# Thirteen kinds of head groups placed with no dense slice in front of them, in a one-core hybrid recurrent decoder step

## The reference, cut to what matters

```python
# layer 0: gated DeltaNet (8 heads) || GLA (4 heads); layer 1: Mamba-2 SSD (16 heads) || RG-LRU (1024 channels)
for li in range(DEPTH):
    xn = _rmsnorm(h, w['norm_g'][li])
    u = xn @ w_in                      # one wide input projection of the layer
    y = heads(u, states)               # conv, decay matrices, chunk products, state updates
    h = h + y @ w_out                  # output projection
    gate = jax.nn.sigmoid(_rmsnorm(h, w['ple_norm'][li]) @ w['ple_w_gate'][li])
    h = h + gate * (p[li] @ w['ple_w_proj'][li])
```

## Time and profile before

| | |
|---|---|
| median of 3 runs | 2558.11 us (2557.02 to 2559.59) |
| the profiled execution | 2557.48 us |
| its span | 2555.7 us |
| TensorE busy / VectorE / ScalarE / GpSimd | 2445.7 / 1253.8 / 952.5 / 382.6 us |
| mean granted TensorE clock | 0.986 of full speed |
| DeltaNet heads | about 103 to 744 us of the span |
| GLA heads | about 744 to 1094 us |
| SSD pairs | about 1617 to 1885 us |

### The profile page before, as it was taken

One profiled execution on the slowest core, in us unless ns is written; L12 is line 12 of the kernel. 1 busy time (PEld: TensorE's weight loads), 2 busy tenths in 40 slices (PEclk: granted clock), 3 DMA queues, 4 the chain that ended last, 5 costly groups with the idle time before them and its releaser, 6 DMA issues.

```text
span 2555.7 us, 52677 instructions
## 1 busy us (share of the span) xinstructions
PE 2445.7 (96%) x22783; PEld 2308.7 (90%) x22783; DVE 1253.8 (49%) x2299; ACT 952.5 (37%) x1531; POOL 382.6 (15%) x590
## 2 busy tenths in 40 slices
PE   7999999999999999999999999999999979999996
PEld 6998888888889999889999999988899979999996
DVE  6644554545544654622343455556655562243332
ACT  5423443234433443432342253333344552243222
POOL 3101111010100101111111111222212111111111
PEclk8999999999999999999999999999999989999998
DMA  9333333333343543643233333333344445223221
GB/s 237 98 96 99 107 93 104 91 94 95 106 118 97 154 141 101 195 164 92 87 90 111 106 109 93 110 110 113 107 122 119 143 152 170 84 82 100 79 85 72
DMA packets 382712, 289.13 MB, mean 113 GB/s; under 512 B 25444, under 2 KB 347758, under 8 KB 381969
## 3 DMA queue, kind: packets, MB, share of 16 engines
q1 hardware_dynamic: 341424, 172.53, 24.9%
q0 software_dynamic: 24640, 81.69, 10.1%
q10 hardware_dynamic: 16416, 31.55, 3.4%
HBM read 229.15 MB, written 57.28 MB: 112 GB/s over the span
## 4 chain that ended last, share of the span: by engine, by line
PE 83%; DVE 5%; ACT 4%; DMA 4%; issue 2%; POOL 0%; SPq 0%; ACTq 0%; DVEq 0%; POOLq 0%
PE psd L562 67%; PE psw L585 2%; PE psw L584 2%; PE psw L605 1%; PE psw L655 1%; PE psw L590 1%; DMA raws<-uT_scratch 1%; PE psw L633 1%; DMA w_raw<-in_ab_w_in_dram 1%; DMA uT_scratch<-mix 1%; PE psw L641 1%; DVE arena L1926 1%; DMA mix<-in_x_prompt_dram 1%; PE psw L627 1%; DMA yT_scratch<-extra 1%
## 5 line engine op out<-in xcount | busy, mean ns | idle before, releaser
L562 PE MATMUL psd<-xh,w_hi 128*128 128x272 f32 x5056 | 1110.7, 301 | 27.7 <-DVE xl L1718 15.4
L562 PE MATMUL psd<-xh,w_lo 128*128 128x272 f32 x5056 | 1051.6, 290 | 0.0
L562 PE MATMUL psd<-xl,w_hi 128*128 128x272 f32 x5056 | 1049.8, 289 | 0.1
L562 PEld LDWEIGHTS psd<-xh,w_hi 128*128 128x128 f32 x5056 | 800.3, 190 | 83.9 <-issue 42.9
L562 PEld LDWEIGHTS psd<-xl,w_hi 128*128 128x128 f32 x5056 | 800.6, 190 | 0.0
L562 PEld LDWEIGHTS psd<-xh,w_lo 128*128 128x128 f32 x5056 | 796.7, 190 | 0.2 <-issue 0.2
L1664 DVE TENSOR_TENSOR w_lo<-w_raw,w_hi 128x512 fp32r<-128x512 f32 x632 | 437.7, 708 | 416.0 <-ACT w_hi L1121 415.0
L1121 ACT CAST w_hi<-w_raw 128x512 fp32r<-128x512 f32 x632 | 377.9, 615 | 671.6 <-PE psd L562 565.2
L2519 POOL TENSOR_TENSOR states<-states,extra 128x544 f32<-128x544 f32 x59 | 80.0, 1356 | 524.8 <-ACT extra L1176 524.8
L2453 POOL DMA_DIRECT2D raws<-uT_scratch x59 | 36.5, 619 | 635.9 <-DMA uT_scratch<-mix 541.6
L2332 DVE TENSOR_TENSOR extra<-psd,rstd 128x544 f32<-128x544 f32 x32 | 23.2, 724 | 156.2 <-PE psd L562 139.2
(11 more groups left out here) (510 smaller groups left out, 2320.7 us busy)
## 6 DMA issues: line engine op xcount, KB each, us to landing
w_raw<-in_ab_w_in_dram SPq DMA_DIRECT2D x224, 256.0 KB, 3.0
w_raw<-in_cd_w_in_dram SPq DMA_DIRECT2D x148, 256.0 KB, 3.2
w_raw<-in_ple_w_gate_dram SPq DMA_DIRECT2D x128, 256.0 KB, 3.1
uT_scratch<-mix ACTq DMA_DIRECT2D x85, 272.0 KB, 2.5
w_raw<-in_ab_w_out_dram SPq DMA_DIRECT2D x64, 256.0 KB, 2.9
w_raw<-in_cd_w_out_dram SPq DMA_DIRECT2D x64, 256.0 KB, 3.0
raws<-uT_scratch POOLq DMA_DIRECT2D x40, 272.0 KB, 3.2
hT_scratch<-arena POOLq DMA_DIRECT2D x8, 1088.0 KB, 10.7
```

The lines of the kernel that those rows point to most:

```text
L562: mm = pe.matmul(out[:, D0 + HALF * half:D0 + HALF * (half + 1)], w[:, r, k % QH, :], x[:, k, HALF * half:HALF * (half + 1)], start=(k == ...
```

## The change

Thirteen kinds of groups get the weight 0 in the sharing of slices. Their target is then that of the group in front of them, so they follow it with no dense slice between. There are 71 such groups: 5 in each of 8 DeltaNet heads, 3 in each of 4 GLA heads, 2 in each of 8 SSD pairs, and 3 in `bc`. Starts and ends of the units stay where they are, and so does the number of slices and of all instructions. The slices taken from in front of these groups go to the other groups of the same unit in proportion to their weights. The order of the groups is unchanged.

```diff
+TOGETHER = {("dn", "ssk"), ("dn", "bbc"), ("dn", "qk"), ("dn", "vt"), ("dn", "ys"), ("gla", "v0"), ("gla", "o1"), ("gla", "sb1"),
+            ("ssd", "dmB"), ("ssd", "ys"), ("bc", "bts"), ("bc", "cb1"), ("bc", "cb3")}
...
                 mine = [n for (v, n, _, _) in GROUPS if v == u]
-                weight = [FILL.get((u, n), FILL.get((u[0], n), 1.0)) for n in mine]
+                weight = [0.0 if (u[0], n) in TOGETHER else FILL.get((u, n), FILL.get((u[0], n), 1.0)) for n in mine]
```

## The result

The changed kernel takes 2560.36 us (median of 20 runs), the kernel before 2556.14 us (median of 20 runs beside them): ratio 1.0021, 95% interval 1.0011 to 1.0030, so 5.4 us slower, from 2.8 to 7.7 (the medians themselves lie 4.2 us apart). The profiled execution took 2561.76 us with a span of 2559.9 (before: 2557.48 and 2555.7). The forecast was +6.8 us. But the sum behind it is not the sum in the trace: single terms are off by up to 5 us and cancel. That the total landed so close is luck.

The account below looks back on a forecast made before the run. TensorE, busy 96% of the span, was taken as the bound, so its order of work counts. Terms -1.8 + 4.5 + 2.1 - 0.5 + 2.5 = +6.8 us gave 2564.9 against the median; range 2557.5 to 2572.

Parts of the forecast that it names:

- joints: Term for all 71 joints between groups: only tiling changes, 0.1 us each, are saved; -1.8 us, bounds 0 and -14.2.
- selector: SSD pairs 2, 4, 6: ebc loses two slices of cover, so three waits for selp grow 1.5 us each; +4.5 us.
- DeltaNet's waits: DeltaNet heads: new t1 waits and odd-head losses against the x5 and x6 waits going; +2.1 us, from -2.8 to +6.
- waits of GLA and of the output projection's first slices: GLA heads: waits at l0 and o0 go, sb0 and the projection's first slices wait longer; -0.5 us, -2.2 to +2.
- clock: Half-rate clock after longer selector waits: one new low stretch (+1.3), one longer (+1.2); +2.5 us, from 0 to +7.
- Four `sb0` with `sb1` stay in one narrow tiling and save both changes, 0.2 each: GLA heads: each of four pairs saves two tiling changes of 0.1 us; 0.8 us in all.
- Eight `ss` with `ys` of SSD go from one narrow tiling to another and save one of two, 0.8: SSD pairs: each of eight joints saves one tiling change of 0.1 us; 0.8 us in all.
- The odd heads lack most of this: 4 x 0.7 = +2.8: Odd DeltaNet heads: they lack most of the 0.7 us by which kk is free sooner in even heads; +2.8 us.
- ScalarE stores the last gate tile in its fill towards `sA`; so the store, the reload ... come some 3 us later: Last GLA head: sA moves from 914 to 919, delaying store, reload and readers of o0 and o1 some 3 us.
- The losses pay each other: Rival for the total: t1 does not wait and the clock does as before; 2557.5 us, chance 0.33.
- Each joint pays: Rival for all 71 joints: each saves an entry and an exit of 0.1 us; 2552.5 us, chance 0.07.
- Two buffers are too few: Rival: a third group waits for the first's delayed reader in most heads, 8 to 10 us more; 2572 and above, chance 0.07.

Follow-up runs that it names:

- e5: Changed kernel with sb0 and sb1 of the GLA heads both on array rows 0 to 63, half the state update left out; one execution, 2562.42 us.
- e3: Kernel before, with only the two SSD kinds (dmB, and ys of SSD) put together; ratio 1.0029 against the kernel before, +7.4 us.
- e7: Changed kernel with 1.0 added to SSD's first weight, so ebc stands 10 slices behind n instead of 7; ratio 0.9988 against the kernel before.
- e9: Kernel before, with only the five DeltaNet kinds put together; ratio 0.9988 against the kernel before, 3.1 us faster.
- e2: Changed kernel without the two SSD kinds, which take their weights of before; ratio 1.0000 against the kernel before.
- e1: Kernel before, with only sb1 of the GLA heads put right behind its preceding group (4 pairs); ratio 1.0007 against the kernel before, +1.8 us.
- e10: Changed kernel, with GpSimd's multiply of the states in the last GLA head held until VectorE finished the state sums; ratio 0.9995 against the kernel before.
- e4: Changed kernel with the second group's weight added to the first, so pairs stand at the second's old place; ratio 0.9982 against the kernel before.
- e8: All pairs at the second's old place, except sb0 with sb1 at sb0's place; ratio 0.9980 against the kernel before, 5.1 us faster.
- e6: Changed kernel with pairs at the first's old place, the second's weight going to the group behind; ratio 0.9965 against the kernel before, 8.9 us faster.

## Why the prediction was right, and where its steps were not

**What bounds the kernel: right.** TensorE's order decides; every effect found is a joint or a wait on it, or the clock behind a wait.

**The sum: close by luck.** Between the two profiled executions, slices 168 to 1799, the terms come to this, in the forecast's own division (the clock's is an estimate: half of the low stretches outside waits):

| term | forecast | in the traces |
|---|---|---|
| joints | -1.8 | -7.0 |
| selector | +4.5 | +3.7 |
| other waits of SSD | 0 | +2.7 |
| DeltaNet's waits | +2.1 | -1.5 |
| waits of GLA and of the output projection's first slices | -0.5 | +2.6 |
| clock | +2.5 | +4.5 |
| sum | +6.8 | +5.0 |

The slices themselves say +5.0. DeltaNet's short waits for "issue" (-0.9 between these two) stand in no term, so the list is good to about a microsecond. The forecast had the joints and DeltaNet 8.8 us too high and the other terms, taken together, 7.0 too low.

**The joint: -1.8 forecast, about -7.0 in the trace (4.5 + 0.6 + 0.5 + 1.4).** The step "Four `sb0` with `sb1` stay in one narrow tiling and save both changes, 0.2 each" failed. A pair saves 1.13 us, four of them 4.5 instead of 0.8. I priced the entry and the exit of a group and took its matmuls as fixed. That `sb0` and `sb1` use different 32-row strips of the array could be read in `state_updates`, and that strips run side by side from the row itself: four matmuls of 512 columns in 1.13 us, where each is listed with 0.64 us on average. The price of being back to back, apart from the strips, was 0.27 to 0.40 by e5, for the 0.2 forecast. For other pairs the time from slice to slice, less the 0.75 of a slice, gives nothing inside the pair (`kt` with `v0` 1.83 us for 1.78 apart, `o0` with `o1` 5.00 for 4.92) and 0.1 outside it, the slow slice behind a group. GLA heads 0 to 2 gain 5.2: 3.4 by `sb`, 1.1 by the wait of `l1` of head 0, which the forecast had (it named `l0`), and the rest, 0.6, by the slices around the joints. The next 0.5 is `bc`'s (slices 940 to 1557).

The last 1.4 is SSD's. There the step "Eight `ss` with `ys` of SSD go from one narrow tiling to another and save one of two, 0.8" failed too: the step from 32*64 to 64*32 inside the pair costs nothing, so both changes are saved. Apart, with the slices beside them and less 0.75 a slice, the two groups take 1.97 us; together 1.77, and 1.84 in the three pairs where `ys` waits. Pair 2 of the changed kernel, from TensorE's timeline:

```profile
1705.19 1.07 PE L658 MATMUL psw<-extra,arena 32*64 32x512 f32 x4
1706.20 0.64 PE L644 MATMUL psw<-states,arena 64*32 64x256 f32 x8
```

**The selector: +4.5 forecast, +3.7 in the trace.** The mechanism was right, and e3 and e7 show it from both sides. The waits were forecast at 4.0, 4.4 and 5.5:

```profile
1690.43 0.55 PE L587 MATMUL psw<-rowR,selp 128*128 128x256 f32 x1 [4.03 <-POOL selp L2629]
...
1763.48 0.36 PE L587 MATMUL psw<-rowR,selp 128*128 128x256 f32 x1 [4.48 <-POOL selp L2629]
...
1835.65 0.55 PE L587 MATMUL psw<-rowR,selp 128*128 128x256 f32 x1 [4.57 <-POOL selp L2629]
```

Only the third is short, by 0.9. It was already the odd one of before, 3.95 us behind the same nine slices.

**What I costed at nothing in SSD: +2.7.** `ys` right behind `ss` needs the buffer that the reader of `sP` frees, three slices on where there were five or, in pair 7, six. It waits 0.82, 0.71 and 0.74 us in pairs 3, 5 and 7, and an `i`, behind the reader of `ss`, 0.44. I had not read the length of that reader, in four pieces (1733.08 to 1736.47 us for pair 3).

**DeltaNet: +2.1 forecast, -1.5 to -2.9 found, -3.1 timed in e9.** `t1` (+4.9 forecast, +4.4), `x5` (-4.6) and `x6` (-0.6 for -1.0) came out, and one `y5` added 0.6. The step "The odd heads lack most of this: 4 x 0.7 = +2.8" failed. `ssq`, `gbc`, `dm` and `kk` together wait 18.9 us (3.9 + 8.0 + 7.0) for 20.2 before (6.2 + 4.4 + 9.6). The odd heads 1, 3, 5 and 7 wait 9.6 us for 11.3, where +2.8 was forecast; the even ones 9.4 for 9.0. So in odd heads too the wait at `ssq` is not simply passed on. Part of the 2.9 is of another kind: the list of waits has short ones that the profile puts down to "issue", 0.9, 2.6 and 2.9 us in this stage in the executions placed as before, 0 to 1.8 in the six placed as in the change. Whether the placement has to do with that stays open; without them the means differ by 1.4 us.

**GLA and the output projection: -0.5 forecast; about 0 in the slices, made of -5.2 and +5.2 with joints and clock in them; +2.6 in waits alone.** The step "ScalarE stores the last gate tile in its fill towards `sA`; so the store, the reload ... come some 3 us later" failed. ScalarE's timeline has that store before the copy of `v1`:

```profile
1065.12 0.33 ACTq L1132 DMA_DIRECT2D uT_scratch<-mix  x1
...
1065.48 0.69 ACT L1348 COPY arena<-psw 128x640 f32<-128x640 f32 x1 [1.88 <-DVE mix L1686]
```

`v1` stands at 912 instead of 907, so the fill that contains the store is the one towards `v1`. Before, the same store and the multiply behind it stood here:

```profile
1072.21 0.33 ACTq L1129 DMA_DIRECT2D uT_scratch<-mix  x1
...
1076.73 3.64 POOL L2601 TENSOR_TENSOR states<-states,arena 128x2048 f32<-128x2048 f32 x1
```

The store came 7 us sooner, not 3 us later. The 0.83 in front of `o0` is absent here, as forecast, but e2 and e7, placed alike, have 1.17 and 1.18 there. The profile puts this wait down to "issue" in every execution that has it, so nothing shows that cover ends it. And the earlier store brought two things forward that had lain in quiet time: ScalarE's 1.88 us wait for the eviction, now ahead of the splits of the projection's input, and GpSimd's multiply, from 1076.73, when VectorE was idle, to 1068.98, into those splits. TensorE waits 1.75, 1.48 and 0.21 us, and falls to half clock. With `qk`'s 1.4 us, by the mechanism of e1, these waits are most of what the last head and the first slices of the projection lost. "+0.4" for the first slices was the cost of an engine's delay. The cost of a collision was not in it. e10 shows the multiply's share; the eviction's share was not tried by itself.

**The clock: +2.5 forecast, +4.5 in this pair of executions, and not to be had closer.** In SSD it is +2.6, at the output projection +1.9. By the means of the placements in the table it is +1.9 and +1.2. The stretches of the changed kernel, beside the earlier trace rows:

```profile
1689.00:1695.70 6.70, 5.27 (x23) 5.30 (x24) 0.69 (x1) 3.59 (x5) 3.62 (x9) 0.50 0.56 161
1764.10:1767.40 3.30, 3.30 (x16) 3.30 (x16) 0.26 (x1) 3.27 (x5) 0.93 (x2) 0.50 0.62 194
1835.80:1839.10 3.30, 3.30 (x15) 3.30 (x16) 0.72 (x1) 2.59 (x4) 1.40 (x2) 0.50 0.46 144
1074.60:1077.90 3.30, 3.30 (x15) 3.30 (x16) 3.23 (x7) 1.50 (x2) 0.00 (x0) 0.50 0.27 79
```

The second selector wait has got its low stretch, as forecast, and the first has a stretch twice as long, of which 1.4 us lie under the wait and 5.3 under work. But the same waits give other stretches in other executions. The kernel before, e2 and e9 have SSD placed alike and the same three waits within 0.04 us (2.53, 2.91 and 3.95 us before). 1.2 GHz shows at two of them in the kernel before, at all three in e2 and at one in e9, and the stage takes 277.1, 279.4 and 275.5 us. e4 and e8 have SSD placed alike and nearly equal waits (2.48, 2.96, 3.21 and 2.55, 2.98, 3.29); e4 has 1.2 GHz at the first of them alone, e8 at all three. The second and third in either:

```profile
1757.50:1760.90 3.40, 3.40 (x33) 3.04 (x33) 0.00 (x0) 2.98 (x4) 1.96 (x3) 1.00 0.64 183
1826.10:1829.50 3.40, 3.40 (x33) 3.04 (x33) 0.00 (x0) 2.95 (x4) 1.40 (x2) 1.00 0.64 198
```

```profile
1755.80:1762.50 6.70, 5.76 (x28) 5.47 (x32) 0.00 (x0) 3.69 (x5) 3.57 (x11) 0.50 0.56 164
1827.50:1834.20 6.70, 6.14 (x32) 5.55 (x32) 0.00 (x0) 3.69 (x5) 2.33 (x5) 0.50 0.45 132
```

The stage takes 273.1 us in e4 and 278.7 in e8. A gap in matmuls puts the clock at risk, and the fall is not certain; 0 to 3 us a wait is what these rows support. The forecast's upper bound, +7 for three stretches of 5.9 us, was mis-summed: half of 17.7 less the 3.4 already lost is about +5.5.

**The rivals.** "The losses pay each other" was wrong in its reason: `t1` did wait. "Each joint pays" came true for two kinds in thirteen, `sb1` by a mechanism of its own and `ys` of SSD with 0.2. "Two buffers are too few" was the `ys` wait of SSD, at 2.3 us and not 8. The sign "`kk` behind `qk` taking less than 2.4 us together" came out as 2.66 (4.03 less the wait of 1.37), against 2.67 before: no price there. Of the other signs, `t1`'s wait in seven heads and none of `x5` came true, `gbc`, `bbc` and `dm` wait 1.7 us a head for the 2 forecast, and `x6` kept 0.4 us where none was forecast.

## What to carry to other kernels

Putting two groups together is two changes at once: the joint, and the cover that the move takes from whatever follows. Keep the first at its old place and give the freed slices to the follower (e6: 8.9 us faster; e4, with both at the second's place, 4.6 us, which the intervals hardly part from it), rather than spreading them over the head (the change: 5.4 us slower). Before pricing neighbours by their tiling, look at which strips of the array their matmuls use: here two groups on different strips cost one, not two. And when a placement moves, follow every engine whose fill ends at it, since what starts sooner can meet what it used to miss.

## What was not expected of the hardware

- Two groups of 32x512 matmuls on different 32-row strips take 1.14 us together and 1.99 us on the same strips (e5).
- VectorE's subtractions with two inputs in SBUF, 0.7 us each, took 5.17 and 4.71 us for two where GpSimd's multiply of 128x2048 (3.6 to 3.9 us) ran beside them, and 1.35 us where it did not (e10).
- Selector waits that are equal to 0.1 us go with none or with 6.7 us of 1.2 GHz from one execution to the next (e4, e8). The stage takes 273.1 and 278.7 us, a difference as large as the effect of the whole change.
- A change of tiling costs 0.1 us against 128*128, and nothing between 32*64 and 64*32 (`ss` with `ys`).
